# The low half of a shared activation buffer moved by 64 bytes in on-chip memory

## The reference

```
z = jnp.einsum("bsd,de->bse", rmsnorm(x, g_mix[i]), w_in[i])
u = jax.nn.relu(jnp.einsum("bsd,df->bsf", h2, w_up[i]))
x = x + jnp.einsum("bsf,fd->bsd", u * u, w_down[i])
gu = h @ w_in                                   # swiglu, d_ff 2816, in both later blocks
...
return (jax.nn.silu(gu[..., :D_FF_2]) * gu[..., D_FF_2:]) @ w_out
```

## Time and profile before

| | us |
|---|---|
| median of 3 runs | 2164.01 |
| lowest and highest run | 2163.43, 2165.67 |
| the profiled execution: its time | 2162.32 |
| the profiled execution: its span | 2160.5 |

### The profile page before, as it was taken

How to read it: one execution, slowest core, us unless ns; L and a number is a source line. 1 busy time by engine, 2 the same in 40 slices (tenths; PEclk the granted TensorE clock), 3 DMA queues, 4 the chain that set the end, 5 groups by cost and what they waited for, 6 DMA issues and landing times. The chain is left out here.

```text
span 2160.5 us, 26090 instructions
## 1 busy us (share of the span) xinstructions
PE 2095.5 (97%) x10710; PEld 1697.5 (79%) x10710; DVE 1146.3 (53%) x1706; ACT 816.6 (38%) x1169; POOL 38.4 (2%) x34
## 2 busy tenths in 40 slices
PE   8999999999999999999999999999999899999998
PEld 6876678888888887787878888887786577888886
DVE  5674765542542579888846444324634736444423
ACT  4324753331232465542534222213325734322212
POOL 0120000000000000000100000000000000000000
PEclk9999999999999999999999999999999999999999
DMA  4220012223223222233122222222240031222221
GB/s 177 86 83 35 2 59 99 94 95 109 85 96 103 91 81 100 108 117 97 40 98 74 95 95 94 95 96 95 98 173 23 1 118 59 98 98 98 98 98 68
DMA packets 43111, 190.68 MB, mean 88 GB/s; under 512 B 15520, under 2 KB 16224, under 8 KB 22384
## 3 DMA queue, kind: packets, MB, share of 16 engines
q1 hardware_dynamic: 40656, 184.78, 25.0%
q10 hardware_dynamic: 2336, 4.23, 0.6%
HBM read 185.25 MB, written 3.74 MB: 87 GB/s over the span
## 5 line engine op out<-in xcount | busy, mean ns | idle before, releaser
L250 DVE TENSOR_TENSOR weights_low<-weights_raw,weights_high 128x2048 fp32r<-128x2048 f32 (+1 forms) x161 | 365.8, 2272 | 565.4 <-ACT weights_high L223 565.3
L441 PE MATMUL psum<-split,weights_high 128*128 128x512 f32 x1448 | 568.3, 392 | 8.3 <-PEq L146 4.2
L442 PE MATMUL psum<-split,weights_high 128*128 128x512 f32 x1448 | 564.6, 390 | 0.0
L443 PE MATMUL psum<-split,weights_low 128*128 128x512 f32 x1448 | 564.6, 390 | 0.0
L223 ACT CAST weights_high<-weights_raw 128x2048 fp32r<-128x2048 f32 (+1 forms) x161 | 304.0, 1888 | 545.3 <-PE psum L443 504.7
L441 PEld LDWEIGHTS psum<-split,weights_high 128*128 128x128 f32 x1448 | 272.2, 188 | 70.3 <-issue 8.4
L443 PEld LDWEIGHTS psum<-split,weights_low 128*128 128x128 f32 x1448 | 272.0, 188 | 57.4
L442 PEld LDWEIGHTS psum<-split,weights_high 128*128 128x128 f32 x1448 | 272.0, 188 | 56.0
L443 PE MATMUL psum<-hidden_high,weights_low 128*128 128x512 f32 x256 | 99.6, 389 | 0.0
L441 PE MATMUL psum<-hidden_high,weights_high 128*128 128x512 f32 x256 | 99.6, 389 | 0.0
L442 PE MATMUL psum<-hidden_low,weights_high 128*128 128x512 f32 x256 | 99.6, 389 | 0.0
(11 more groups left out here) (485 smaller groups left out, 3081.4 us busy)
## 6 DMA issues: line engine op xcount, KB each, us to landing
weights_raw<-in_weights SPq DMA_DIRECT2D x161, 1024.0 KB, 4.9
minus_c<-minus_c_rows ACTq DMA_DIRECT2D x16, 256.0 KB, 7.3
x_stream<-in_x SPq DMA_DIRECT2D x4, 512.0 KB, 7.1
gdn_in_grown<-gdn_rows SPq DMA_DIRECT2D x4, 512.0 KB, 4.7
chain_grown<-gdn_rows SPq DMA_DIRECT2D x4, 512.0 KB, 3.7
out<-end_results SPq DMA_DIRECT2D x8, 256.0 KB, 2.1
table<-rope_tables SPq DMA_DIRECT2D x1, 1024.0 KB, 12.0
weights_raw<-in_weights SPq DMA_DIRECT2D x1, 768.0 KB, 4.2
```

The costliest lines, as they stand in the source:

```text
L250: self.nc.vector.tensor_tensor(out=self.low_of(n)[:, 0:width], in0=self.raw[:, n % 2, 0:width], in1=self.high_of(n)[:, 0:width].bitcast(se ...
L441: nc.tensor.matmul(bank, wh, ah, start=first, stop=False)
L442: nc.tensor.matmul(bank, wh, al, start=False, stop=False)
L443: return nc.tensor.matmul(bank, wl, ah, start=False, stop=last)
```

## The change

The low half of `split` begins 16 floats (64 bytes) later. The buffer is declared with rows of 8 x 512 + 16 floats, and the old view is cut out of it. The low half's address goes from 119936 to 120000, its phase from 128 to 192; the high half stays at 103552. So that nothing above overlaps, everything placed at 64 KB or higher goes up by 128 floats, which is 512 bytes, and keeps its phase. No instruction is added or removed, none changes its place on its engine, and all shapes stay.

```diff
+LIFT, LOW_LIFT = 128, 16
...
     def place(name, at, shape, dtype=mybir.dt.float32):
 
-        under = int(at * 256)
+        under = int(at * 256) + (LIFT if at >= 64 else 0)
...
-        gates, split = place("gates", 0, [P, 2 * DT, T]), place("split", 32, [P, 2, DT, T], f32r)
+        gates, split_home = place("gates", 0, [P, 2 * DT, T]), place("split", 32, [P, 2, DT * T + LOW_LIFT], f32r)
+        split = split_home[:, :, 0:DT * T].rearrange("p s (k t) -> p s k t", k=DT)
         block_one(gates, split)
```

## The result

The changed kernel takes 2191.17 us (median of 4, 2186.31 to 2192.88) where the kernel before, with its runs beside these, takes 2163.72: a ratio of 1.0123, 95% interval 1.0104 to 1.0141. It is 27 us slower. The profiled execution took 2186.31 us, with a span of 2184.5, 24.0 us over the span of before. The profiled execution had a mean granted clock of 0.989, the other three runs of the changed kernel (2190.27 to 2192.88 us) one of 0.984 to 0.985, so a few of the 27 us may be clock and not pitch.

What follows compares the result with a forecast made beforehand. The prediction took TensorE's matmul count times pitch as the bound. Every term was 0, summing to 0 on the profiled 2162.32 us, so the forecast median was 2164.0 us, with an 8-in-10 range of 2150 to 2188.

Steps and rivals of the forecast that it cites:

- What bounds the kernel, and where an address could act: TensorE's matmuls, 97% of the span; an address could act only on the 0.0133 us each costs over its columns.
- So the distance between the two streams does not set the extra: Matmuls streaming `split`: moving-to-stationary phase distance was said not to cause the 0.0133 us over columns; term taken as 0.
- Row group 6: Profile rows with stationary columns at phase 384, distance 256: 16 matmuls at 0.2269 us, read as the usual pitch.
- Row group 7: Profile rows with 80 stationary columns, distance given as 192: 15 matmuls at 0.2267 us, read as the usual pitch.
- Rows 8: Profile stretch with 16 stationary columns and stepping phases: 0.2312 us, 4.5 ns more, read as the matmuls' own rhythm.
- rival A: All 4824 matmuls streaming `split`: alternating phase unsettles the stream, 4.5 ns each, 21.7 us slower, 2186 us; chance 0.19.
- VectorE's writes: 72 instructions writing the low half: at most 8 ns each, 0.6 us if all on the path; taken as 0.
- the stationary use of the low half: 128 matmuls where tokens are stationary and weights move: stationary phase said to cost nothing, taken as 0.
- the lift: 512 bytes for everything at 64 KB and above, phases modulo 512 kept: taken as 0, with a small chance left.
- rival B: Streams of `split`: a start 64 bytes off reduces the extra, 2154, 2143 or 2123 us; 450 matmuls or more; chance 0.18.
- the 0.0133 us at distance 0: What every matmul at full clock costs over its 512 columns; the forecast thought it may come from moving-operand reads.

Runs made afterwards that it cites:

- low_256: Changed kernel, but the low half of `split` begins 256 bytes further on (phase 384) in place of 64: 2166.68 us, ratio 1.0012 to the kernel before.
- both_64: Kernel before with the 512-byte lift and both halves of `split` moved by 64 bytes to phase 192: 2175.80 us, ratio 1.0056.
- both_192: Kernel before with the 512-byte lift and both halves of `split` moved by 192 bytes to phase 320: 2193.46 us, ratio 1.0127.
- weights_64: Kernel before with all three weight buffers and small constants moved by 64 bytes to phase 192, activations left at 128: 2206.47 us, ratio 1.0197.
- all_64: Kernel before with every buffer, weights and activations, moved by 64 bytes to phase 192: 2163.31 us, ratio 1.0003.
- lift_only: Changed kernel without the low half's 64 bytes; everything at 64 KB and above still 512 bytes higher: 2163.77 us, ratio 1.0007 to the kernel before.
- both_96: Kernel before with the 512-byte lift and both halves of `split` moved by 96 bytes: 2197.84 us, ratio 1.0162, two runs.
- both_160: Kernel before with the 512-byte lift and both halves of `split` moved by 160 bytes: 2196.13 us, ratio 1.0154, two runs.
- low_128: Changed kernel, but the low half of `split` begins 128 bytes further on (phase 256) in place of 64: 2185.27 us, ratio 1.0102 to the kernel before.
- wlow_64: Kernel before with `weights_low` and the small constants behind it moved by 64 bytes to phase 192, `split` untouched: 2194.82 us, ratio 1.0135.

## Why the prediction was wrong

*What bounds the kernel, and where an address could act:* right. The time is the pitch times the count, the loss is the pitch's, and 23.1 us of it sit on the 4824 matmuls that were counted, all three of each product.

*The step that failed* is "So the distance between the two streams does not set the extra", drawn from rows 6 and 7. Row group 6 has a distance of 256, which low_256 shows to be the same as 0. Row group 7 has 128 - 320 = -192, which is 64 modulo 256, the mildest of the seven, and with 80 stationary columns and not 128. Two points of a periodic dependence, taken without knowing the period, were read as a flat line. In its place, for 128 stationary columns, both_64 (0.2289 us at a constant 64), both_192 and weights_64 (0.2333 at -64, from either side) and all_64 (0.2267 with every phase moved together) show that the distance decides and a common shift does not.

The stretch of rows 7 could not have told this, as the other traces show. In lift_only both of its operands are at the very addresses of before, and the same 15 matmuls take 0.2307 us each where before they took 0.2267. In both_192 they are at distance 0, and take (1557.80 - 1554.30) / 15 = 0.2333 us; in weights_64, at distance 0 too, 0.2327:

```profile
1554.30 0.39 PE L444 MATMUL psum<-split,weights_low 128*80 128x512 f32 x1
...
1557.80 0.39 PE L444 MATMUL psum<-split,weights_low 128*80 128x512 f32 x1
```

So with 80 stationary columns the prices are others, distance 0 is not the good one, and one set of addresses can give two pitches. Rows 7 showed one of the two.

*Rows 8 were put aside* because durations alternated by two while addresses stepped by three. That was a weak reason against the only rows that showed a higher pitch: a stream can have a rhythm of its own and still be set going by the addresses. Stepping isn't needed for a loss, though: in both_96 the distance is constant, and the pitch is 0.2335 us. The six products of rows 8 step through the distances 128, 64, 0, 192, 128 and 64 modulo 256; at the prices of 128-column loads that would be 0.2305 us in the mean, an estimate from the constant distances above, against the 0.2312 of the rows. So they may have shown the distance all along, but with 16-column loads this is not shown, and lift_only has 0.2321 there with every phase kept. They had about the right size: 0.2312 us was expected of rival A, 0.2319 was measured in the window, and its 21.7 us against 23.1 for the same matmuls is 6% under. That this came so near is in part luck. Rival A's mechanism was a pattern that shifts from matmul to matmul, and a shift by 256 costs nothing (low_256), while a distance that never changes costs up to 7.6 ns (both_160).

*VectorE's writes, the stationary use of the low half, the lift:* the first and the last cost nothing, as worked out (L1092 at 744 ns; lift_only at 1.0007). The second was taken as 0 and is not: with tokens stationary, the changed kernel is slower too, on 384 matmuls (128 products), whose pitch goes from 0.2267 to 0.2311 us in their unbroken stretches. It comes to 1.6 us in the trace.

*The range* ended at 2188 us, at rival A's price and 2 us more. That left little for an error in the price or for the granted clock: the median lies 3 us beyond, while the profiled execution, 2186.31 us at the highest clock of the four, lies inside. The sign given for rival B, 450 matmuls or more, would also have missed its milder half: 10.4 us less over 4824 matmuls is 447.

**What stays open** is the rule by which two streams disturb each other: which load meets which moving operand, why a distance of 64 in one matmul of three costs more on all three than 64 in all of them, what picks one of several pitches at the same phases (low_128, and the 80-column stretch), and where the 0.0133 us at distance 0 come from. That two reads collide is a picture and was not shown. Shown is that with 128 stationary columns the cost hangs on the distance, repeats after 256 bytes, has a sign, can be set off from either side, and is there at full clock alone.

## What to carry to other kernels

When a kernel lives on a steady stream of float32-reduced matmuls at full clock, with 128 stationary columns, compare the addresses of stationary and moving operands modulo 256 and keep them equal, in all buffers that take part; here every layout tried that did not keep them equal cost 0.6 to 2.0% of the whole. With fewer stationary columns, measure: in the 80-column stretch distance 0 was among the slow ones. A filler that looks like waste may be what keeps that true, so a new small buffer in front of an arena wants its size rounded up to 256 bytes. And when a trace shows a quantity to be flat in an address at two or three points, ask which period would make these points the same one.

## What the runs showed of the hardware that was not expected

With 128 stationary and 512 moving columns at full clock, TensorE's pitch is 0.2267 us at distance 0 and 256 and 0.2289 to 0.2343 us at seven other distances in steps of 32 bytes; moving every buffer by 64 bytes changes nothing (all_64). At half clock it is 0.4267 at all of them, its columns alone. Alternating between distance 0 and 64 (the change, 0.2319) is worse than a constant 64 (both_64, 0.2289), alternating between 0 and 256 (low_256) is free. With 80 stationary columns the order of the distances is another (0.2333 us at distance 0 in both_192), and the same addresses gave 0.2267 and 0.2307 (before and lift_only). The Trainium skill ("SBUF — State Buffer", "SBUF: two separate sides") says that TensorE and ScalarE never wait on anyone. That speaks of one engine and another, and no run here tests it; the loss seen here hangs on TensorE's own two operands. The Trainium skill ("TensorE: Matmul & The Clock Gate", part 2, step 1) also says that loading the next tile's weights doesn't steal read bandwidth from the running matmul. For this stream the runs speak against it: wlow_64 moved nothing but `weights_low` and small constants, and matmuls that stream unmoved activations became longer by up to 9 ns. Whether it is bandwidth that is lost was not measured.
